# Attention of the first layer: which operand of the value product is held in TensorE, and where its result is divided by the row sums

## The reference, cut to what matters

```python
# A: 8 query heads, 2 kv heads, window of the chunk and the two before it
scores = einsum(q, k) / 8, masked;  probs = softmax(concat([scores, sink]))[..., :-1]
ya = einsum(probs, v) * silu(ag)
# B: 8 heads, all chunks before and its own
scores = einsum(q, k) / 8 + bias, masked;  probs = softmax(scores)
yb = einsum(probs, v) * silu(bg)
x = x + concat([ya, yb]) @ w_out
```

## Time and profile before

| | us |
|---|---|
| median of 3 executions | 1969.12 (1969.1 to 1969.15) |
| the profiled execution | 1970.39 |
| its span in the profile | 1968.6 |
| PE busy | 1930.7 (98%) |
| DVE, ACT, POOL busy | 1023.3, 1004.8, 948.8 |

### The profile page before, as it was taken

One profiled execution on the slowest core, in us unless ns is written; L12 is line 12 of the kernel. 1 busy time (PEld: TensorE's weight loads), 2 busy tenths in 40 slices (PEclk: granted clock), 3 DMA queues, 4 the chain that ended last, 5 costly groups with the idle time before them and its releaser, 6 DMA issues.

```text
span 1968.6 us, 26969 instructions
## 1 busy us (share of the span) xinstructions
PE 1930.7 (98%) x10062; PEld 1616.6 (82%) x10062; DVE 1023.3 (52%) x1871; ACT 1004.8 (51%) x1775; POOL 948.8 (48%) x1236
## 2 busy tenths in 40 slices
PE   8999999999999999999999999999999999999997
PEld 7888887877779888888788888888879888888886
DVE  4366445665644777566646644402646484444214
ACT  5466735676744555566436344422656464444223
POOL 4642255545454444444554555555453445555552
PEclk9999999999999999999999999999999999999999
DMA  5321122322222222222222233333222223223332
GB/s 199 97 61 53 54 77 85 91 81 81 80 75 87 75 77 74 84 78 75 77 86 97 91 107 97 94 96 91 83 67 64 75 76 107 97 97 96 91 94 73
DMA packets 55379, 169.33 MB, mean 86 GB/s; under 512 B 7120, under 2 KB 14032, under 8 KB 55120
## 3 DMA queue, kind: packets, MB, share of 16 engines
q1 hardware_dynamic: 54960, 167.50, 27.0%
q10 hardware_dynamic: 288, 0.10, 0.0%
HBM read 158.66 MB, written 2.10 MB: 82 GB/s over the span
## 4 chain that ended last, share of the span: by engine, by line
PE 91%; DVE 5%; ACT 2%; POOL 1%; issue 1%; DMA 0%; SPq 0%; ACTq 0%; DVEq 0%; POOLq 0%
PE ps L1897 23%; PE ps L1900 23%; PE ps L1898 23%; PE ps L1966 3%; PE ps L1951 3%; PE ps L1909 3%; PE ps L1912 3%; PE ps L1910 3%; PE ps L1959 2%; PE ps L1935 1%; PE ps L1945 1%; PE ps L2049 1%; POOL wl L2640 1%; PE ps L1925 1%; PE ps L1924 1%
## 5 line engine op out<-in xcount | busy, mean ns | idle before, releaser
L2640 POOL TENSOR_TENSOR wl<-st,wh 128x256 fp32r<-128x256 f32 (+1 forms) x1180 | 879.8, 777 | 962.9 <-ACT wh L2073 962.4
L1897 PE MATMUL ps<-xh,wh 128*128 128x512 f32 x1432 | 581.5, 406 | 4.6 <-ACT tmp L2103 3.0
L1900 PE MATMUL ps<-xh,wl 128*128 128x512 f32 x1432 | 559.3, 391 | 0.1
L1898 PE MATMUL ps<-xl,wh 128*128 128x512 f32 x1432 | 558.4, 390 | 0.0
L2073 ACT ACTIVATE wh<-st 128x1024 fp32r<-128x1024 f32 (+2 forms) x311 | 314.2, 1011 | 437.1 <-PE ps L1900 389.3
L1897 PEld LDWEIGHTS ps<-xh,wh 128*128 128x128 f32 x1432 | 269.2, 188 | 62.1 <-issue 5.8
L1900 PEld LDWEIGHTS ps<-xh,wl 128*128 128x128 f32 x1432 | 268.7, 188 | 58.6 <-POOL wl L2640 0.5
L1898 PEld LDWEIGHTS ps<-xl,wh 128*128 128x128 f32 x1432 | 269.5, 188 | 53.3 <-issue 4.1
L2599 DVE SCALAR_TENSOR_TENSOR tmp<-ps,vec,tmp 128x510 f32<-128x510 f32 (+1 forms) x176 | 131.2, 749 | 206.2 <-ACT tmp L2252 203.3
L2557 DVE SCALAR_TENSOR_TENSOR res<-res,ps 128x512 f32<-128x512 f32 (+1 forms) x37 | 22.7, 614 | 219.1 <-PE ps L1900 211.1
L1897 PE MATMUL ps<-fa_h,wh 128*128 128x512 f32 x308 | 119.8, 389 | 0.0
(11 more groups left out here) (286 smaller groups left out, 3395.3 us busy)
## 6 DMA issues: line engine op xcount, KB each, us to landing
st<-in_f_up SPq DMA_DIRECT2D x88, 512.0 KB, 3.3
st<-in_o_fm SPq DMA_DIRECT2D x32, 512.0 KB, 3.6
st<-in_s_xbc SPq DMA_DIRECT2D x32, 512.0 KB, 3.6
st<-in_f_dn SPq DMA_DIRECT2D x32, 512.0 KB, 3.5
st<-in_e_fm SPq DMA_DIRECT2D x21, 512.0 KB, 3.6
st<-in_s_z SPq DMA_DIRECT2D x16, 512.0 KB, 3.5
st<-in_s_out SPq DMA_DIRECT2D x16, 512.0 KB, 3.4
tmp<-tmp SPq DMA_DIRECT2D x100, 64.0 KB, 2.0
```

Source lines behind the costliest of these rows:

```text
L1897: e.matmul(u.bank.ap, hi, x.h[:, kk, :], start=first, stop=False)
L1898: e.matmul(u.bank.ap, hi, x.l[:, kk, :], start=False, stop=False)
L1900: e.matmul(u.bank.ap, lo, x.h[:, kk, :], start=False, stop=last).then_inc(S["mm"], 1)
L2640: e.tensor_tensor(P.mem["wl"][w.m % NWR][:, part], P.mem["stage"][w.m % NSTAGE][:, part], P.mem["wh"][w.m % NWR][:, part].bitcast(F32), AL ...
```

## The change

In the first layer, `pv` exchanges its operands: the values (128x64) are held and the transposed probabilities (128x128) streamed. The result is feature-major: head 0 in partitions 0 to 63, head 1 in partitions 64 to 127, 128 columns for each `i`. Both heads of a pair are flipped and multiplied in one step, two key blocks at a time. So the result needs no transpose; instead a new task `roots` takes the sums once the four `exp` are done, inverts them, spreads each over 64 columns in an SBUF tile (`o_n`, now a copy), transposes that (`feat`, now into an `aux` bank) and multiplies it into the gate (`y_g`, first use). `finish` is left with one multiplication of the `ob` bank by the scaled gate (`y_g`, second use) and the split. `roots` waits for the gate ahead of `o_n`. The planner's length of a first-layer product is 112 ns (it was 167); for the odd layer and the latent attention, whose `pv` and `feat` calls are only written anew, it stays 224.

```diff
@@ -269,7 +269,7 @@
         if kind == "flip":
             return 109 * n
         if kind == "pv":
-            return (224 if o[2] > 64 else 167) * len(o[5])
+            return o[3] * len(o[1])
         if kind == "u_mm":
             return 430 * o[4]
         if kind in ("exp", "flip_a", "head_hi", "u_in"):
@@ -1008,6 +1008,7 @@
     qs, ks = ring(mem["qz"]), ring(mem["kz"])
     rl, pr, pts = ring(mem["small"]), ring(mem["pr"]), ring(mem["e_pt"])
     got = {}
+    scaled = [None] * 8
     negsink = lambda fb: mem["bro"][:, B_OFF["sink"] + fb:B_OFF["sink"] + fb + 5:4]
 
     def bias():
@@ -1068,7 +1069,7 @@
                 P.start(5, gates.bring(j, u))
         rt.extend((yield from outputs(P, y, lambda j: [T["e_out"][j]], evac, norm, third, halves=2)))
 
-    def finish(fb, ob, mn, sm, ends):
+    def roots(fb, mn, sm, ends):
         if fb < 4:
             sx = yield from P.taken(rl)
             t = yield ("sink_x", sx, mn.ap, negsink(fb), ends + [tneg])
@@ -1076,39 +1077,50 @@
             t = yield ("sums", sm.ap, sx.ap, [t] + ends)
             sx.release(t)
             ends = ends + [t]
+        mn.release(ends)
         t = yield ("rec", sm.ap, ends)
-        o = yield from P.taken(P.tmp)
-        t = yield ("o_n", o, ob, 64, sm.ap, ends + [t])
-        mn.release(t)
-        sm.release(t)
-        f = yield ("feat", ob, o, t)
-        o.release(f)
         while gates.t[fb] is None:
             yield lambda: gates.t[fb] is not None
+        o = yield from P.taken(P.tmp)
+        t = yield ("o_n", o, None, 64, sm.ap, [t])
+        sm.release(t)
+        bank = yield from P.taken(P.aux)
+        f = yield ("feat", bank, [cols(o.ap, i) for i in range(4)], t)
+        o.release(f)
+        gate = Use(Slot(gates.sg[:, fb, :]))
+        scaled[fb] = yield ("y_g", gate, bank, None, gate.ap, f, gates.t[fb])
+        bank.release(scaled[fb])
+
+    def finish(fb, ob, done):
+        while scaled[fb] is None:
+            yield lambda: scaled[fb] is not None
         v = yield from P.taken(P.tmp)
-        e = yield ("y_g", v, ob, None, gates.sg[:, fb, :], f, gates.t[fb])
+        e = yield ("y_g", v, ob, None, gates.sg[:, fb, :], done, scaled[fb])
         ob.release(e)
         yt[fb] = yield from P.split_g(v.ap, yH[:, fb, :], yL[:, fb, :], [e], [])
         v.release(yt[fb])
 
-    def back(fb, i, kb0, halves, tiles, ob, mn, sm, ends):
+    def back(fb, i, kb0, halves, tiles, ob, done):
         nb = halves.n // 128
-        for hs in ([(0, 1)] if halves.small else [(0,), (1,)]):
-            pt, t = yield from P.flip_g([cols(halves.p[hh], b) for hh in hs for b in range(nb)], nb * len(hs),
-                                        [tiles[hh].expd for hh in hs], pts)
-            if hs[-1]:
+        for b0 in range(0, nb, 2):
+            bs = range(b0, min(b0 + 2, nb))
+            pt, t = yield from P.flip_g([cols(halves.p[hh], b) for b in bs for hh in range(2)], 2 * len(bs),
+                                        [a.expd for a in tiles], pts)
+            if b0 + 2 >= nb:
                 for u in halves.p_uses:
-                    u.release(t, *([] if halves.small else [t0]))
-            t0 = t
-            for at, hh in enumerate(hs):
-                vs = [va[:, kb0 + b, hh * 64:hh * 64 + 64] if fb < 4 else
-                      vb[:, kb0 + b, (2 * fb - 8 + hh) * 64:(2 * fb - 7 + hh) * 64] for b in range(nb)]
-                t = yield ("pv", ob, (2 * i + hh) * 64, 64, [pt.ready, tv],
-                           [cols(pt.ap, at * nb + b) for b in range(nb)], vs)
-                ends.append(t)
+                    u.release(t)
+            parts = []
+            for at, b in enumerate(bs):
+                for hh in range(2):
+                    v = (va[:, kb0 + b, hh * 64:hh * 64 + 64] if fb < 4 else
+                         vb[:, kb0 + b, (2 * fb - 8 + hh) * 64:(2 * fb - 7 + hh) * 64])
+                    parts.append((ob.ap[64 * hh:64 * hh + 64, i * 128:i * 128 + 128], v, cols(pt.ap, 2 * at + hh),
+                                  b == 0, b == nb - 1))
+            t = yield ("pv", ob, parts, [pt.ready, tv], 112)
             pt.release(t)
-        if len(ends) == 16:
-            P.start(2, finish(fb, ob, mn, sm, ends))
+        done.append(t)
+        if len(done) == 4:
+            P.start(2, finish(fb, ob, done))
 
     def attend():
         while len(tv) < 5 or len(tb) < 8:
@@ -1157,7 +1169,8 @@
                     ends.append(e)
                 for u in g.uses:
                     u.release(*(a.expd for a in tiles))
-                P.start(1, back(fb, i, kb0, g, tiles, ob, mn, sm, ends))
+                P.start(1, back(fb, i, kb0, g, tiles, ob, done))
+            P.start(3, roots(fb, mn, sm, ends))
 
     y = Acts(yH, yL, 8)
     yt = y.t
...
@@ -1959,18 +1972,18 @@
                 t = e.transpose(cols(tb.ap, k), part, ident)
             t.then_inc(S["flip"], 1)
         elif kind == "pv":
-            ob, c, n, ready, pts, vs = o
+            ob, parts, ready, _ = o
             pe.freed(ob)
             pe.wait_ge(ready)
-            for j, (pt, v) in enumerate(zip(pts, vs)):
-                t = e.matmul(ob.ap[:, c:c + n], pt, v, start=(j == 0), stop=(j == len(vs) - 1),
-                             skip_group_check=True)
+            for out, held, moved, first, last in parts:
+                t = e.matmul(out, held, moved, start=first, stop=last, skip_group_check=True)
             t.then_inc(S["pv"], 1)
         elif kind == "feat":
-            fb, ot, normed = o
-            pe.wait_ge(normed)
-            for i in range(4):
-                t = e.transpose(cols(fb.ap, i), cols(ot.ap, i), ident)
+            bank, parts, ready = o
+            pe.freed(bank)
+            pe.wait_ge(ready)
+            for i, part in enumerate(parts):
+                t = e.transpose(cols(bank.ap, i), part, ident)
             t.then_inc(S["feat"], 1)
         elif kind == "va_t":
             bank, vf, ready = o
@@ -2376,8 +2389,11 @@
             out, ob, n, r, ready = o
             dve.wait_ge(ready)
             dve.freed(out)
-            e.tensor_tensor(blocks(out.ap, n), blocks(ob.ap, n),
-                            r.unsqueeze(2).to_broadcast([128, 512 // n, n]), ALU.mult).then_inc(S["o_n"], 1)
+            r = r.unsqueeze(2).to_broadcast([128, 512 // n, n])
+            if ob is None:
+                e.tensor_copy(blocks(out.ap, n), r).then_inc(S["o_n"], 1)
+            else:
+                e.tensor_tensor(blocks(out.ap, n), blocks(ob.ap, n), r, ALU.mult).then_inc(S["o_n"], 1)
         elif kind == "y_g":
             y, ob, gain, gate, turned, ready = o
             dve.wait_ge(turned)
```

More of the change, by code:

```diff
@@ L1122, in attend @@
             mn, sm = (yield from P.taken(rl)), (yield from P.taken(rl))
-            ends = []
+            ends, done = [], []
             for i in range(4):
@@ L1242, in finish @@
         rr.release(t2)
-        f = yield ("feat", ob, o, [t2, ends])
+        f = yield ("feat", ob, [cols(o.ap, i) for i in range(4)], [t2, ends])
         o.release(f)
@@ L1256, in back @@
         g.p_uses[0].release(t)
-        t = yield ("pv", ob, i * 128, 128, [pt.ready, tv[h]], [cols(pt.ap, b) for b in range(nb)],
-                   [v[:, b, h * 128:(h + 1) * 128] for b in range(nb)])
+        t = yield ("pv", ob, [(cols(ob.ap, i), cols(pt.ap, b), v[:, b, h * 128:(h + 1) * 128], b == 0, b == i)
+                              for b in range(nb)], [pt.ready, tv[h]], 224)
         pt.release(t)
@@ L1767, in finish @@
         sm.release(t)
-        f = yield ("feat", ob, o, t)
+        f = yield ("feat", ob, [cols(o.ap, i) for i in range(4)], t)
         o.release(f)
@@ L1776, in back @@
         p.release(t)
-        t = yield ("pv", ob, i * 128, 128, [pt.ready, tv], [cols(pt.ap, b) for b in range(nb)],
-                   [v[:, b, h * 128:(h + 1) * 128] for b in range(nb)])
+        t = yield ("pv", ob, [(cols(ob.ap, i), cols(pt.ap, b), v[:, b, h * 128:(h + 1) * 128], b == 0, b == i)
+                              for b in range(nb)], [pt.ready, tv], 224)
         pt.release(t)
```

## The result

The changed kernel took 1965.76 us (median of 16 executions, 1964.34 to 1966.88); the kernel before, run beside it, 1970.05 us (16 executions, 1968.94 to 1971.14). The forecast was 1965.6 with a range of 1961.5 to 1970.5.

A forecast was written before the change was run, and what follows sets the result against it. The prediction took PE's work in order plus one wait at the layer's end as the bound. Products 1.8 us and the end 1.7 us gave 3.5 us less, from 1969.12 to 1965.6, with an 8-in-10 range of 1961.5 to 1970.5.

The forecast's parts named there:

- The bound: First layer's attention: time is PE's work in order, 175 of 178 us busy, plus one wait at the layer's end.
- Price of a record and of a step: Value products: 0.0544 us a record plus 0.35 a step; 8 records 0.90 to 0.79 us, 4 records 0.45 to 0.57.
- The products' sum: All 272 value-product records in 40 steps: 30.6 us falls to 28.8, gain 1.8 us (1.0 to 3.4).
- Rival 3: Value-product steps beside 128-column work pay a higher fee, 0.73 us: 1980.8 for all, 1973.2 for half; chance 9%.
- The end of the layer: Behind the last value product, inverse sums done earlier: last-split wait 2.2 to 0.5 us, gain 1.7 us (0 to 2.2).
- The transposes, VectorE, the banks: First layer: as many transposes, cost 0 on PE; added DVE work and `aux` bank use covered, costed at nothing.
- Pair 6: Pair 6 begins up to 2.7 us later behind the longer gate chain; 4.8 us of room, so cost 0.
- 1: Value products at half price without the step fee: PE saves 15.8 us, with the end 17.5, giving 1951.6; chance 6%.
- 4: Pair 6 too late: delay 7 us in place of 2.7, 2.2 beyond the room, giving 1967.8 or more; chance 6%.
- 2: Layer's end doesn't gain, as the planner sees cheaper products and orders the tail otherwise: only 1.8 us, 1967.3; chance 19%.

The follow-up runs named there:

- e1: Changed kernel, but each value product holds all 128 value columns and writes all 128 partitions, so no column halves; 1968.85 us, ratio 0.9996 to the kernel before.
- e3: Changed kernel, but both heads of a step write the same 64-partition half, so products can't run side by side; 1978.65 us, ratio 1.0046 to the kernel before.
- e4: Changed kernel, but `roots` (inverse sums, scaled gate) starts only when a pair's last value product is planned; 1972.41 us, ratio 1.001 to the kernel before.
- e9: Between e6 and e7: a block's two flips run side by side for the last pair only; 1964.54 us, ratio 0.9973 to the kernel before.
- e7: From e6: the two flips of a block with three or four key blocks no longer wait for each other; 1972.6 us, ratio 1.0012 to the kernel before.
- e5: Changed kernel, with the planner told 350 ns a step beside 112 ns a product, only order can differ; 1965.99 us, ratio 0.9979 to the kernel before.
- e8: From e7: products of several query blocks share a step, 20 steps in place of 32; 1961.03 us, ratio 0.9953 to the kernel before.
- e6: Changed kernel, with all value products of a block in one step after its flips, 32 steps for 40; 1966.03 us, ratio 0.9979 to the kernel before.
- e2: Changed kernel, with products inside a step issued head by head in place of alternating; 1965.92 us, ratio 0.9978 to the kernel before.

## Why the prediction was right, step by step

**The bound.** Right. All the difference lies in the stretch, in TensorE's work and its waits. Stretch 3.7 us shorter: work 172.7 to 170.7, waits 2.6 to 0.9.

**Price of a record and of a step.** Right to the digit: 0.79 and 0.58 us for 8 and 4 records, against 0.79 and 0.57. e1 and e3 show what the two parts of it are: 0.109 us a pair because of the two halves, and 0.35 us for entering and leaving.

**The products' sum.** Right in size: 1.8 us was forecast, TensorE's work fell by 2.0. Two small errors in it cancel. The price of entering and leaving is 0.36 us where 0.35 was taken, 0.4 us more over 40 steps. And the steps are not "each alone": in one place two stand side by side, 12 records in 1.01 us, and pay it once.

```profile
179.07 0.39 PE L1913 MATMUL ps<-xh,wl 128*128 128x512 f32 x1
179.38 0.88 PE L1979 MATMUL ps<-e_pt,e_vb 128*64 128x128 f32 x12
...
180.53 0.39 PE L1911 MATMUL ps<-xl,wh 128*128 128x512 f32 x1
```

Against e1 the work differs by 2.6 us, not 2.0. TensorE's list is the same record by record there, and the 39 distances from the record ahead of a group to the second behind it differ by 2.8 us in sum. But 0.6 of the work is e1's own, for its products stream 128 columns where those before streamed 64. Beside projections both cost 0.90 us for 8 records. With four transposes behind them (8 records and 4) the three kernels, before, e1 and changed, show:

```profile
95.82 0.39 PE L1900 MATMUL ps<-xh,wl 128*128 128x512 f32 x1
96.05 1.00 PE L1966 MATMUL ps<-e_va,e_pt 128*128 128x64 f32 x8
...
97.56 0.39 PE L1898 MATMUL ps<-xl,wh 128*128 128x512 f32 x1
```

```profile
249.55 0.39 PE L1913 MATMUL ps<-yh,wl 128*128 128x512 f32 x1
249.78 1.05 PE L1979 MATMUL ps<-e_pt,e_vb 128*128 128x128 f32 x8
...
251.34 0.40 PE L1911 MATMUL ps<-yl,wh 128*128 128x512 f32 x1
```

```profile
245.38 0.40 PE L1913 MATMUL ps<-yh,wl 128*128 128x512 f32 x1
245.70 0.66 PE L1979 MATMUL ps<-e_pt,e_vb 128*64 128x128 f32 x8
...
247.02 0.40 PE L1911 MATMUL ps<-yl,wh 128*128 128x512 f32 x1
```

Less 0.45 that is 1.29, 1.34 and 1.19 us. So from before to changed the step gains 0.10 us beside transposes too, against 0.11 alone, and e1 pays 0.05 more than before. 19 of its 39 groups have transposes right behind; by an estimate from these rows that is some 0.9 us, enough for the 0.6. Rival 3, a higher fee beside short products, did not come.

**The end of the layer.** Right, and the mechanism is shown by e4. The wait fell from 2.2 to 0.6 us, 1.6 where 1.7 was forecast, and the chain behind the last product took the 2.13 us that the sum gave it. The wait for a normed query, which the forecast left alone, fell from 0.5 to 0.3. So the stretch's 3.7 us are 2.0 of products, 1.6 of the last wait and 0.2 of the other, against a sum of 1.8 and 1.7. What is luck is the last digit: a single stretch can be off by a us (e9), and the medians differ by 4.3.

**The transposes, VectorE, the banks.** No wait for `aux` or `e_pt` came up. `o_n` as a copy takes 0.47 us in the mean where I bounded it by 0.69. That `aux` has little to spare was seen only in e7.

**Pair 6.** Its first score came 117.9 us behind the first score of all, before 118.6: the longer chain behind the gate was covered. The last pair began 1.8 us after its key's split ended, before 1.9, still led by the key.

**Rivals.** 1 fell by the price of a step, 3 by the steps beside transposes, 4 by the times of pair 6, and 2 by the last wait, which went, and by e5, where the true price moved the stretch by 1.1 us.

## What to carry to other kernels

Swapping held and streamed operands to use both halves of the columns halves a small product's price only while the step is long: with a fee of 0.36 us a step, 4 short products just pay (0.90 to 0.79 us), 2 lose, 8 gain (1.80 to 1.24). Read the fee from a step of the same form that the trace already has, from the product ahead to the second behind, and then gather products into few steps: that was worth more (4.7 us of time from the changed kernel to e8) than the exchange itself (2.0 us of work). And move what hangs only on sums or norms ahead of the last product of a layer, where its latency is bare.

## What the runs showed of the hardware

- Entering and leaving products with 64 held columns costs 0.36 to 0.37 us a step beside projections, for 4, 8, 12 and 16 records alike (0.58, 0.79, 1.01, 1.24 us; changed kernel and e6), seen on the load path as 0.34 us of idle time that no semaphore ends. The Trainium skill, TensorEngine Tiling (Array Packing), Key Properties, has the drain as a rule; the 32 places above agree with it, and e3 adds that one half used alone pays it too.
- Two records on different halves start 0.005 to 0.014 us apart in the traces, also when the list brings four for one half and then four for the other (e2). On one half alone they stand 0.109 us apart (e3).
- Around waits of 0.9 and 2.9 us that follow each other TensorE's granted clock was 0.52 from 256 to 263 us (e4), behind waits of 0.3 and 1.6 us 0.57 from 246 to 250 us (e7); in the changed kernel, with waits of 0.3 and 0.6 us far apart, it was 1.00 from 80 to 255 us. The same list of instructions waited 0.3 us in one execution and 1.6 in another at the same place (e6, e9), and the first score, ahead of which nothing was changed, stands 2.7 us apart between executions, in the order of the granted clock from 10 to 20 us.
